# A later gate row, moved position sums, and one key tile and one head's values of a cross attention made at the end of the attention before it

## What is computed

```
for i in range(2):                                      # first block
    h = modulate(rmsnorm(x, norm_g[i, 0]), sh1, sc1)
    x = x + 0.5 * g1 * swiglu(h, ffn_w13[i, 0], ffn_w2[i, 0])
    h = modulate(rmsnorm(x, norm_g[i, 1]), sh2, sc2)
    m = pool_ssd_mixer(h, ...) if i == 0 else mla_mixer(h, ...)
    x = x + g2 * m
    h = modulate(rmsnorm(x, norm_g[i, 2]), sh3, sc3)
    x = x + 0.5 * g3 * swiglu(h, ffn_w13[i, 1], ffn_w2[i, 1])
x = rmsnorm(x, final_norm_g)

h = rms_norm(x, norm_mix_g)                             # second block
x = x + hybrid_mixer(h, ...)
h = rms_norm(x, norm_x_g)
x = x + cross_attention(h, mem, wq, wkv, wo)
h = rms_norm(x, norm_ffn_g)
x = x + swiglu_2(h, ffn_in_w, ffn_out_w)
return rms_norm(x, final_norm_g)
```

```
def hybrid_mixer(h, ...):
    (u_conv, q, kc, vc, ks, vs, kw, vw, g_heads, g_conv, g_attn) = split(h @ w_in)
    conv_out = conv_module(u_conv, ...)     # depthwise conv, layer norm, silu, @ pw_w
    nsa_out = nsa_attention(q, kc, vc, ks, vs, kw, vw, g_heads, cmp_pos, ...)
    y = sigmoid(g_conv) * conv_out + sigmoid(g_attn) * nsa_out
    return y @ w_out

def compress_blocks(blocks, pos, w1, w2):   # inside nsa_attention, for kc and vc
    z = blocks + pos
    z = einsum("bnlgd,lde->bnge", z, w1)    # the part of pos is the position sum
    return silu(z) @ w2

def cross_attention(h, mem, wq, wkv, wo):   # 4 heads of 256, mem has 256 rows
    q = h @ wq
    k, v = split(mem @ wkv, 2)
    p = softmax(q @ k.T / 16)               # by head
    return (p @ v) @ wo
```

## Time and profile before

| | us |
|---|---|
| median of 3 runs | 1765.22 |
| fastest and slowest run | 1764.48, 1767.01 |
| profiled execution | 1766.82 |
| its span, from first to last instruction | 1764.7 |
| PE busy in it | 1670.6 (95%) |
| DVE busy | 1287.9 (73%) |
| ACT busy | 931.2 (53%) |
| POOL busy | 92.5 (5%) |

### The profile page before, as it was taken

The page is one execution under the profiler, slowest core; times in us unless marked ns, Lnnn a source line. Parts: engine busy times, 40 slices in busy tenths (PEclk is TensorE's granted clock), DMA queues, the critical chain, the costliest instruction groups (busy, mean ns, idle before and its releaser), DMA issues.

```text
span 1764.7 us, 31721 instructions
## 1 busy us (share of the span) xinstructions
PE 1670.6 (95%) x11182; PEld 1500.5 (85%) x11182; DVE 1287.9 (73%) x2157; ACT 931.2 (53%) x1662; POOL 92.5 (5%) x162
## 2 busy tenths in 40 slices
PE   6899999898999999999999899989999899999998
PEld 5799989888999889999777788889997688988886
DVE  6888888768888888876556466669969666456665
ACT  1544457644444544445566455563648765555553
POOL 2000010300000100000001000010000000000000
PEclk9999999999999999999999999999989999999999
DMA  9888877757888788867443766644553246446661
GB/s 350 304 297 297 301 181 203 158 203 269 304 298 303 234 296 304 296 182 234 143 117 98 209 188 184 190 149 146 154 149 109 66 144 200 144 136 199 191 186 63
DMA packets 125304, 360.88 MB, mean 205 GB/s; under 512 B 10026, under 2 KB 53562, under 8 KB 115488
## 3 DMA queue, kind: packets, MB, share of 16 engines
q1 hardware_dynamic: 108128, 262.18, 47.2%
q10 hardware_dynamic: 12432, 78.65, 13.7%
q0 software_dynamic: 4656, 18.87, 3.2%
HBM read 352.42 MB, written 7.23 MB: 204 GB/s over the span
## 4 chain that ended last, share of the span: by engine, by line
PE 74%; DVE 14%; ACT 6%; issue 4%; DMA 1%; POOL 1%; ACTq 0%; DVEq 0%; POOLq 0%; SPq 0%
PE ps L877 52%; PE ps L1218 9%; PE ps L1219 4%; DVE w_lo L229 4%; DVE arena L2862 2%; ACT w_hi L223 2%; DVE arena L384 1%; DVE resid L1495 1%; DMA raw<-in_stream 1%; PE ps L464 1%; DMA arena<-in_small 1%; PE ps L451 1%; PE ps L739 1%; PE ps L394 1%; DVE tmp L1492 0%
## 5 line engine op out<-in xcount | busy, mean ns | idle before, releaser
L877 PE MATMUL ps<-t_both,w_hi 128*128 128x256 f32 x3844 | 708.8, 286 | 7.8 <-DVE arena L2836 4.4
L877 PEld LDWEIGHTS ps<-t_both,w_hi 128*128 128x128 f32 x3844 | 600.0, 191 | 20.4 <-issue 8.7
L877 PE MATMUL ps<-t_both,w_lo 128*128 128x256 f32 x1922 | 544.5, 283 | 1.2 <-issue 1.2
L229 DVE TENSOR_TENSOR w_lo<-raw,w_hi 128x1024 fp32r<-128x1024 f32 x240 | 288.2, 1222 | 122.2 <-ACT w_hi L223 121.9
L1287 DVE TENSOR_TENSOR w_lo<-raw,w_hi 128x1024 fp32r<-128x1024 f32 x258 | 313.6, 1221 | 81.6 <-ACT w_hi L1276 81.6
L877 PEld LDWEIGHTS ps<-t_both,w_lo 128*128 128x128 f32 x1922 | 367.5, 191 | 0.2
L1276 ACT ACTIVATE w_hi<-raw 128x1024 fp32r<-128x1024 f32 x258 | 268.3, 1053 | 112.8 <-PE ps L877 73.0
L223 ACT ACTIVATE w_hi<-raw 128x1024 fp32r<-128x1024 f32 x240 | 247.5, 1052 | 146.4 <-PE ps L877 99.7
L1218 PE MATMUL ps<-t_both,w_hi 128*128 128x512 f32 x640 | 226.8, 398 | 0.0
L877 PE MATMUL ps<-w_hi,g_hi 128*128 128x512 f32 x440 | 178.0, 405 | 20.6 <-DVE g_lo L1367 18.4
L1219 PE MATMUL ps<-t_both,w_lo 128*128 128x256 f32 x640 | 179.7, 281 | 0.0
(11 more groups left out here) (395 smaller groups left out, 1773.0 us busy)
## 6 DMA issues: line engine op xcount, KB each, us to landing
raw<-in_stream SPq DMA_DIRECT2D x498, 512.0 KB, 4.5
arena<-in_mod_w ACTq DMA_DIRECT2D x72, 1024.0 KB, 7.2
grow<-gate_scratch POOLq DMA_DIRECT2D x6, 512.0 KB, 7.1
u_scratch<-u_keep ACTq DMA_DIRECT2D x1, 3072.0 KB, 36.4
mem_scratch<-arena_for_products POOLq DMA_DIRECT2D x1, 2048.0 KB, 11.0
arena<-u_scratch POOLq DMA_DIRECT2D x8, 256.0 KB, 3.3
arena_for_products<-mem_scratch POOLq DMA_DIRECT2D x1, 1536.0 KB, 7.1
small<-in_small POOLq DMA_DIRECT2D x1, 1368.0 KB, 11.5
```

The costliest lines, as they stand in the source:

```text
L229: VE.tensor_tensor(w_lo[:, s, :], raw[:, s, :], w_hi[:, s, :].bitcast(F32), ALU.subtract).then_inc(lo_done, 1)
L877: last = TE.matmul(out, lhs, rhs, start=start and i == 0, stop=stop and i == 2)
```

## The change

- `gate_row` takes a number of blocks, `behind`, that must have been used before POOL starts. For FFN3 it is 30 blocks from the FFN's first; for the others 0.
- In `squares` for the hybrid norm one of the two `w_lo` is paid ahead of the diagonal and not behind it; and one is paid ahead of the residual add at the end of the latent attention.
- The position sums go from the heads 6 and 7 of the latent attention to the start of `states()` in the state-space mixer, with bank ps1, and ACT copies them there.
- `pass_rows` becomes `pair_rows`: one inverse and one multiplication for the sums of two passes.
- Key tile 7 and the value blocks of head 0 are put between the last turns of the passes and behind them. The ring order takes blocks 407 and the first two value blocks there; the memory is loaded back in parts beside the passes; `keep_busy` in front of the pointwise product goes. The three splits owed by it, and the copies of the keys and values, stand behind `conv_split`.
- The value weights are read by head: a block is then four pieces of 256 columns of four row tiles, and its products are eight triples of 256 columns in two banks, where they were four of 512 in four banks. Head 1 to 3 stay behind the norm, six blocks, with the x transposes behind the first and second of them.

```diff
-AHEAD = {LATENT_IN: (0, 1), FOURTH_FFN: (2, 3), HYBRID_IN: (4, 5, 6)}
+AHEAD = {LATENT_IN: (0, 1), FOURTH_FFN: (2, 3), HYBRID_IN: (4, 5, 6), POINTWISE: (7, 8, 9)}
...
+    if MEM_VALUES <= b < MEM_VALUES + 8:
+        head, half = divmod(b - MEM_VALUES, 2)
+        return MEM_VALUES + 4 * half, head, L
...
+            if splits:
+                pay_lo()
...
-        def gate_row(kind):
+        def gate_row(kind, behind=0):
...
+                pool.wait_ge(used, behind)
                 pool.wait_ge(mod_added, min(N_MOD, kind[0] // 4 + 2))
...
-                    gate_row(residual)
+                    gate_row(residual, behind=h0 + 5 * RING)
...
         def states():
+
+            @block.tensor
+            def _(pe):
+                pe.wait_ge(small_in.sem, small_in.n)
+                for kind in range(2):
+                    for lp in range(16):
+                        last = TE.matmul(ps[1][0:64, 64 * kind:64 * kind + 60], sm("w1", (kind * 16 + lp) * 64, (kind * 16 + lp + 1) * 64),
+                                         sm("pos", kind * 16 + lp - 59, kind * 16 + lp + 1), start=lp == 0, stop=lp == 15)
+                last.then_inc(T.sem, T.up())
+            positions_at = T.n
...
-                if h in POSITIONS_AT:
-                    kind = POSITIONS_AT[h]
-                    pe.wait_ge(small_in.sem, small_in.n)
-                    for lp in range(16):
-                        last = TE.matmul(ps[6][0:64, 384:444], sm("w1", (kind * 16 + lp) * 64, (kind * 16 + lp + 1) * 64),
-                                         sm("pos", kind * 16 + lp - 59, kind * 16 + lp + 1), start=lp == 0, stop=lp == 15)
-                    last.then_inc(T.sem, T.up())
...
         hv_of[0] = 2
+        pay_lo()
         add_residual((mod_at(1, 5), 1.0))
...
-                dve.wait_ge(A.sem, exp_done[n])
+                dve.wait_ge(A.sem, exp_done[n + 1])
                 VE.reciprocal(rinv, sums).then_inc(V.sem, V.up())
                 dve.wait_ge(V.sem, V.n)
-                VE.tensor_tensor(rinv, rinv, gates[:, :, c:c + 1].rearrange("p q a -> p (q a)"), ALU.mult).then_inc(V.sem, V.up())
-            weighed[n] = V.n
+                by_pass = rinv.rearrange("p (a q) -> p a q", q=QT)
+                VE.tensor_tensor(by_pass, by_pass, gates[:, :, c:c + 2].rearrange("p q a -> p a q"), ALU.mult).then_inc(V.sem, V.up())
+            weighed[n] = weighed[n + 1] = V.n
...
+        def value_block(head, half, banks, source, ready):
...
+                for q in range(QT):
+                    qs = slice(q * P, (q + 1) * P)
+                    for i in range(4):
+                        k, ws = 4 * half + i, slice(i * L, (i + 1) * L)
+                        last = triple(banks[q][:, 0:L], source(k, 0)[:, qs], source(k, 1)[:, qs], w_hi[:, s, ws],
+                                      w_lo[:, s, ws], False, k == 0, k == KT - 1)
+                last.then_inc(used, 1)
+            owed[0] += 1
...
+            if step == N_PASS:
+                @block.tensor
+                def _(pe):
+                    pe.wait_ge(V.sem, sc_read[N_PASS - 1])
+                    pe.wait_ge(A.sem, fill_free[6])
+                key_tile(ps[2][:, 0:L], mem_ahead, (mem_back, 112))
+            if step == N_PASS + 1:
+                value_block(0, 0, (ps[3], ps[0]), mem_ahead, (mem_back, 112))
...
+        value_block(0, 1, (ps[3], ps[0]), mem_ahead, (mem_back, 112))
+        last_value = blocks["pe"]
...
         for pr in range(4):
             conv_split(pr)
...
+        for _i in range(owed[0]):
+            next_split()
+        owed[0] = 0
...
-                        keep_busy(bank, 9)
+                        pass
...
-        key_tile(ps[4][:, 0:L], mem_again, (mem_back, 96))
...
-        rows_product(KT, D, put_off=True, chained=True, operand=mem_again)
-        meanwhile.clear()
-        evac_rows(vx, ACT.Copy)
+        value_kept = {}
+        for head in range(1, 4):
+            banks = (ps[2], ps[3]) if head == 2 else (ps[0], ps[1])
...
+            for half in range(2):
+                value_block(head, half, banks, mem_again, (mem_back, 128))
+                owed[0] -= 1
+                next_split()
+                turn_beside()
```

More of the change, by code:

```diff
@@ L299, in back_of @@
             def back_of(i):
-                back = {h - at if first is None else None for h, (first, at) in enumerate(order) if h // RING == i}
+                back = {h - at if first is None else None for h, (first, at, _) in enumerate(order) if h // RING == i}
                 return back.pop() if len(back) == 1 else None
@@ L1768, in states, with _ @@
             small_at["state"] = A.n
+            @block.scalar
+            def _(act):
+                act.wait_ge(T.sem, positions_at)
+                E.activation(position_sum, ps[1][0:64, 0:128].rearrange("p (k c) -> p k c", c=64)[:, :, 59],
+                             ACT.Copy).then_inc(A.sem, A.up())
+            position_kept[0] = A.n
         fresh_in = turned["at"] == (V.n, A.n)
@@ L1865, in _ @@
                         pe.wait_ge(A.sem, z_free[pair - 2])
+                    if half == 0 and pair == 1:
+                        pe.wait_ge(A.sem, position_kept[0])
                 for k in range(4 * part, 4 * part + 4):
@@ L3559, in build, with _ @@
         turned["at"] = (V.n, A.n)
[L3562 to L3568 removed]
+        @block.tensor
+        def _(pe):
+            pe.wait_ge(A.sem, memory_kept)
         rows_product(KT, D, put_off=True, tile_of=out_tile)
@@ L3582, in build @@
         x_diag = squares(lambda q: x[:, q, :], dict(x_ready))
-        pay_splits()
-        key_tile(ps[4][:, 0:L], mem_again, (mem_back, 96))
-        last_key = blocks["pe"]
-        @block.scalar
-        def _(act):
-            act.wait_ge(used, last_key)
-            E.activation(kx[:, 7, :], ps[4][:, 0:L], ACT.Copy).then_inc(A.sem, A.up())
         pay_splits()
```

107 lines of the change are left out of this document (69 added, 38 removed).

## The result

| | before | changed |
|---|---|---|
| median, us | 1766.12 (4 runs, 1764.48 to 1771.08) | 1746.51 (4 runs, 1745.18 to 1747.42) |
| profiled execution, its span | 1766.82, 1764.7 | 1747.42, 1745.3 |
| PE busy | 1670.6 | 1660.1 |

The changed kernel takes 0.9884 of the time of before (95% interval 0.9862 to 0.9905), 19.6 us less by the medians. 1746.6 was forecast, from 1765.2 for the kernel before, whose fourth run (1771.08) came with this result; against 1766.1 it would have been 1747.5. The total is right, and yet one reason for its largest term is not: the experiments show that the late gate row, on which 9.2 us were booked, could have been left out.

A forecast was written before the change was run, and what follows sets the result against it. TensorE was taken as the bound, 74% of the chain of work that ended last. Terms of -9.2, -1.1, -1.2, -2.7 and -4.4 sum to -18.6, giving 1746.6 us from the median 1765.2; range 1742.5 to 1756.

The forecast's parts named there:

- late gate row: Fourth FFN's start: moving the 4 KB gate line to mid-loop removes TensorE's stall, -9.2 us, bounds -9.7 and -6.
- the other `pay_lo`: Low half ahead of the residual add before the fourth FFN: 0, with +0.3 us if it outlasts DVE's wait.
- The `g_first` load: 512 KB load left at the fourth FFN's start: might hold part of the stall; last FFN's similar load cited against.
- The low half ahead of the root: Hybrid norm: one `w_lo` fills DVE's 2.53 us of standing, -1.1 us, bounds -1.2 and 0.
- Position sums: -4.0 us in latent attention, +2.8 in the state-space mixer, where a 1.16 us wait covers part: net -1.2.
- Row scales: Sparse attention's passes: DVE sets the pace, 0.27 us saved per pair over 10 pairs, -2.7, bounds 0 and -4.3.
- The tail: Passes' end to queries: +3.1 us until the pointwise product, -7.8 and 0.3 back behind the output product, together -4.4.
- (1): Rival: the fourth FFN's stall moves with the gate line or stays, 1755.8 us; chance 0.12.
- (2, 4): Rivals: clock falls at the pointwise product, briefly (+3.8 us, 1750.4, chance 0.16) or lastingly (+22.8, 1769.4, chance 0.03).
- (3): Rival: paired row scales save nothing because TensorE or ACT paces the passes, +2.7 us, 1749.3; chance 0.12.

The follow-up runs named there:

- e4: Kernel of before with only key tile 7, first head's values at the passes' end, by-head value weights and no constant matmuls: 1761.03 us, ratio 0.9969.
- e11: Changed kernel with the fourth FFN's gate row early again and the latent attention's low half back behind the norm: 1753.37 us, ratio 0.9932.
- e1: Changed kernel with only the fourth FFN's gate row starting at once again: 1745.20 us, ratio 0.9890.
- e12: Changed kernel with only the latent attention's low half back behind the norm, gate row still late: 1744.66 us, ratio 0.9888.
- e6: Kernel of before with only the 512 KB load of the final norm's gain moved behind 30 used blocks: 1761.47 us, ratio 0.9981.
- e5: Changed kernel with both low halves of the hybrid norm back behind the diagonal: 1747.48 us, ratio 0.9907.
- e9: Changed kernel with the convolution's split waiting only for blocks used ahead of the key tile: 1743.28 us, ratio 0.9874.
- e3: Changed kernel with row scales made for each pass by itself again: 1748.46 us, ratio 0.9905.
- e7: Changed kernel with the fourth FFN's 4 KB gate line written twice in mid-loop: 1748.11 us, ratio 0.9903.

## Why the prediction came out as it did

**Late gate row (-9.2, measured -9.3 for the stage): size right, cause half right.** The control with the last FFN gave the price of the stall to 0.1 us in the profiled run, and the line does slow the blocks. That match is in part luck: the same stall measures some 7 us in e4 and e11. What failed is the sentence that booked the other `pay_lo` at 0 because it only "takes the `w_lo` off its list behind the norm". A low half also frees a slot, and its load started 14.5 us earlier; that by itself takes the stall away (e1), as does the late row (e12). Two edits that each suffice look like one in a sum: with the row alone (e12) the term holds, with the half alone (e1) the sum would have been some 7 to 9 us off.

**The `g_first` load** was set aside with the last FFN as a witness; e6 shows that this was no proof, and leaves open how large its part is.

**The low half ahead of the root (-1.1):** as written, 0.99 us left of the wait, and in e5's trace it is 2.13 again.

**Position sums (-1.2, measured -0.9 by the stages).** The 1.16 us of cover are there: the mixer grew by 2.6. The latent attention gave back 3.5 of the 4.0; where the other 0.5 went was not looked into.

**Row scales (-2.7, measured -3.7).** DVE does pace the passes, but not in every pair: 0.5 us in every second one, 2.1 in ten pairs where 0.27 each was taken. The term missed the channel sums, where PE waits for DVE's maximum and its clock is low afterwards: 0.5 us of wait and 1.0 of matmuls. The 1.0 is no sure gain of the edit, for in e1 and e11 the same matmuls take 1.7 us less again.

**The tail (-4.4, measured -4.2; -4.2 for e4).** The wait ahead of the pointwise product is 1.41 against 1.3, the first block ends 3.2 us later and not 3.1 (both counted from the last scores), behind the output product it is 21.0 us to the queries where 20.8 were forecast (20.5 and 0.3), and the clock stayed at 1.00. Why the wait was there was read from the code as a need (that DVE "overwrites what this block reads"). That is wrong: the second value block reads the arena, and e9 takes the wait away.

**The rest** cancels: 1.9 us more at the start, which is how runs differ, and 1.9 less ahead of the first scores, where no edit stands. Neither was foreseen, and the terms' own errors are up to 1.0 us, in both directions. The profiled execution of before, from which the sum was taken, is also none of the three runs, whose slowest took 1767.0 us and not 1766.8. That the sum came within 0.1 us of the median is luck.

**The rivals.** The stall did not move with the line (1): mid-loop blocks took 9.7 us where 12 to 14 were forecast, ACT waited there for no load, and beside two lines blocks took 10.8. The clock (2, 4) did not fall behind 1.41 us. The row scales (3) do save.

## What to carry to other kernels

Where a ring of buffers feeds the engines, the place of a split (the instruction that frees a slot) is a place in the load queue as well: ask of every moved one which load starts with it, and what stood in that load's way. A stall that comes of several things at once can vanish with any one of them; the credit of an edit is then only known with the four corners (both, each, neither), not from a sum. And a wait written as "all blocks so far" grows when new blocks are put ahead of it: aim it at the last reader.

## What the runs showed of the hardware

**The clock's falls come and go between kernels with equal work.** The second half of the 15-column products ahead of the scores took 3.60 us before, in e4, e6 and e11, and 1.96 in the changed kernel and all others, behind the same short waits of at most 0.75 us in the 20 us ahead. In the windows view of the kernel before:

```profile
1305.00:1308.00 3.00, 3.00 (x22) 2.96 (x23) 1.22 (x5) 0.00 (x0) 0.00 (x0) 0.50 0.00 0
```

and of the changed kernel at the same work:

```profile
1295.00:1298.00 3.00, 3.00 (x26) 3.00 (x27) 2.82 (x7) 0.00 (x0) 0.00 (x0) 1.00 0.00 0
```

Half clock (1.2 GHz) in the one and full clock (2.4 GHz) in the other, with PE busy throughout in both. The four kernels with the fall come to this place at 1296.6 us or later, the others at 1293.1 or earlier; whether the moment matters or what preceded it stays open. It made 1.9 us of the 19.4. The one slice of the page with a lower clock before, the 30th of 40, covers 1279 to 1324 us and so this place, not the stage around 1430 us. Behind PE's wait in the passes it is alike: 3.2 us idle are followed by 5.41 us of matmuls in the changed kernel and seven others, and by 3.72 in e1 and e11. The Trainium skill, "TensorE: Matmul & The Clock Gate", Part 1: The HAM clock gate (the "warmup" mystery), says that one kernel has a different number of slow matmuls from run to run. The difference of e1 and the changed kernel, with the same instructions there, could be that; but e1 and e11 are also the two with an early gate row and the new row scales, so another cause isn't excluded, and one profile of each kernel can't show what varies within one.

**Small elements slow the loads beside them.** A store of 1024 elements of 4 bytes took 10.2 (e3, in mid-loop) to 14.3 us (before, at the start of FFN3) from its issue to the read behind it, and 512 KB blocks issued beside one took 9.7 to 14.3 in the median, where without it they took 5.3 to 5.7 at the same place of the FFN (e12 and the changed kernel). A second such line at the same time (e7) made it 15.7 us, 4 to 5 us more than one line takes there, and not the double.
